# A one-layer hybrid recurrent decoder step on one core: x turned for the residual by VectorE, recurrent heads planned a unit sooner, a small product inside unit 1, one state load a slot later

## The chip, the cores and the metric

The kernel runs on one core of one Trainium2 chip. The metric is device time in microseconds for one execution. Three executions of the kernel before took 988.83, 991.7 and 995.17 us, median 991.7.

## What is computed

One step of a one-layer decoder trunk for a prompt of 512 tokens and a sample group of 8 sequences with 4 tokens each, so 544 token columns in all; the model width is 1024, everything is float32.

```python
def _layer(x, st, p):
    xn = rmsnorm(x, p['norm_mix_g'])
    proj = (xn @ p['w_in'] + p['b_in']).astype(f32)
    gq, gk, gv, gg, ga, mu, mi, mf, mo, rx, ry, gates = jnp.split(proj, ...)
    # GLA branch: lg = log_sigmoid(ga @ w_gla_a2 + b_gla_a2) / 16, chunked scan over q, k, v
    o_gla = head_rmsnorm(o, p['gla_norm_g'], 4) * jax.nn.silu(gg)
    # mLSTM branch: conv of mu, q/k/v, stabilised matrix memory C [v, k] for 4 heads
    o_m = head_rmsnorm(hm, p['mlstm_norm_g'], 4) * jax.nn.sigmoid(mo)
    # RG-LRU branch: conv of rx, r_g and i_g block-diagonal gates, linear recurrence
    hr, rh_new = rglru(xc, r_g, i_g, p['rglru_lambda'], rh)
    o_r = hr * jax.nn.gelu(ry)
    g3 = jax.nn.sigmoid(gates).reshape(B, L, 3, D_MODEL)
    mix = sum(g3[:, :, b] * (o_b @ wb_b) for b in range(3))
    x = x + mix @ p['w_out']
    xn2 = rmsnorm(x, p['norm_ffn_g'])
    uc, fconv_new = causal_dwconv(xn2 @ p['w_up'], fconv, ...)
    u_a, u_b = jnp.split(uc, 2, axis=-1)
    return x + (jax.nn.gelu(u_a) * u_b) @ p['w_down'], new_states
```

A final RMSNorm follows, and the new states of all branches are outputs too, for the prompt and for the 8 samples.

## The kernel before

Activations lie with features on the 128 partitions and the 544 tokens in the free dimension. The weights are worked off in **units**, numbered 0 to 120: a unit is one tile of 128 output features. Unit 0 holds the small projections, 1 to 8 q, k and v of GLA, 9 to 12 mu, 13 to 16 rx, 17 to 20 ry, 21 to 24 gg, 25 to 28 mo, 29 to 52 the three branches with their gates (24 units), 53 to 60 w_out (`U_OUT` is 53), then the feed-forward part (`U_UP`, `U_DOWN`).

A product is made of three float32r passes, high by high, low by high, high by low, over 8 tiles of 128 input features: 8 x 3 x 2 halves of 272 tokens = 48 matmuls. A unit of the branches has two products: the gate product (8 tiles, 48 matmuls) into PSUM pair 0, then the branch product (4 tiles, 24 matmuls) into pair 1.

For each unit u the work goes round five queues, each of which is strictly in its written order:
- **SP** loads the weights into one of two stage slots (`load`, L374) once GpSimd is through with unit u-2 (`free_stage`, semaphore `lo`).
- **ScalarE** casts them to the high part `whi` (`hi`, L1122; in loops L1131) once TensorE is through with unit u-2.
- **GpSimd** subtracts to the low part `wlo` (`lo`, L523), three instructions.
- **TensorE** makes the products (`gemm`, L602). Below unit 29 it waits for `evac` of unit u-2, that is, for ScalarE having emptied PSUM.
- **ScalarE** evacuates (`evac`, L1187 on). In the loop over u it does: wait for the product of u, `hi(u + 2)`, `evac(u)`, then the visits of u.

All else (recurrences, states, small products) is put between the units as **visits**: `plan(u, part, (what, k), ...)` says behind which unit (part 0) or between the two products of which unit (part 1) a step stands. Each engine has a function for each kind of step and calls it at that place of its own queue; steps of one unit come in the order in which they were planned. The steps that matter here:
- `a2`: TensorE's small product of `ga` with `wa2` (8 matmuls, L689), behind unit 1; ScalarE's `v_a2` takes its Abs twice (L1228), and then Abs, Exp and Ln of several rows.
- `rg` (TensorE L808 and ScalarE L1329 to L1338) and `rgd` (VectorE L1928 to L1946) for each recurrent head: TensorE makes two block-diagonal products, ScalarE Sigmoid twice, Tanh, Exp, Sqrt, VectorE the scan and the gated output `orh`, `orl`. ScalarE's step of head i waits for head i-1's gated output (`rg_o`); VectorE's raises `or`. Planned at units 24, 26, 28 and, between the products, 30.
- `gfin` (unit 24): VectorE makes the gated output of GLA, `ogh` and `ogl`, and raises `og` (L1904 to L1909); it waits for gg's last evacuation (unit 24). ScalarE stores the GLA states there.
- `rh` (unit 31, part 1): TensorE turns `rhn`, the new states of the recurrent branch, and waits for `or` of all four heads.
- `sH`, `sI` for h = 0 to 3: the sample step of mLSTM head h. `sH`: TensorE turns the state `ch_buf[h % 3]` in PSUM, ScalarE copies it to `cts` (L1418). `sI`: TensorE's products with `cts` (L911 to L915), VectorE's update, ScalarE's store of the new state. There are three buffers for four heads, so head 3's load waits for head 0's store (`ch_out`), in `sH(1)` on ScalarE.

The evacuation of unit 25, the first of mo, waits for `og`:

```python
i = u - U_MO
if i == 0:
    act.wait_ge(s("og"), 1)
    act.wait_ge(s("ss_new"), 2)
ins = func(split(mo[:, i, :]), src, ACT.Sigmoid, ...)   # L1219
```

TensorE begins unit 29 only after `evac` of all 29 units (`pe.wait_ge(s("evac"), U_GB)`).

Between units 53 and 54 TensorE turns x for the residual: x is loaded again in token order (`xp2`, `xs2`), 40 float32 turns go to PSUM pairs 2 and 3, and VectorE copies them to `xt` (L2126), one of eight tiles at a time. Behind the copies VectorE sets `up`, `fraw` and `ssa` to zero (L2127 to L2129). SP waits for `ssa`, loads the feed-forward convolution state into `fraw` (four loads, pieces of 128 bytes, L463), and goes on with the weights of unit 57. From unit 55 on TensorE waits for `x1`, VectorE's sum of `xt` and the product of two units before.

Of the kernel before, what the change touches and what calls it, by code (L numbers as in the profile page):

```python
# [13 lines left out]
P = 128  # L14
# [74 lines left out]
def layer(nc, io):  # L89
    ctx = ExitStack()  # L90
    with ctx:
# [72 lines left out]
        xs2 = at("xs2", [TS, D_MODEL], o)  # L164
# [10 lines left out]
        xp2 = at("xp2", [P, 4, D_MODEL], w0 + 8 * TB)  # L175
# [186 lines left out]
        def _(sp):  # L362
# [70 lines left out]

            for n in range(3):
# [5 lines left out]
                def pair_of_units(i):  # L440
                    for r in range(2):
                        slot = (u0 + r) % 2
                        free_stage(i * 2 + (u0 + r))
                        load(slot, one(gates, i * 2 + r), KT_IN)
                        sp.dma_start(stage[:, slot, KT_IN:KT_GB], one(outs, i * 2 + r)).then_inc(s(f"branch{slot}"), 16)

                done = 0
                if n == 2:
                    done = 2
                    for i in range(done):  # L450
                        pair_of_units(i)
# [134 lines left out]
        def _(pe):  # L586
# [507 lines left out]
        def _(act):  # L1094
# [1231 lines left out]
```

## Time and profile before

| What | Value |
|---|---|
| Median of three executions | 991.7 us (988.83 to 995.17) |
| Profiled execution | 993.07 us, span of its core 991.3 us |
| Mean granted TensorE clock | 0.991 |
| TensorE matmuls | 969.4 us busy, 98% |
| VectorE / ScalarE / GpSimd | 539.4 / 402.8 / 310.8 us busy |
| DMA | 89.62 MB, mean 90 GB/s |
| SP's queue, hardware_dynamic | 154341 packets, 79.16 MB |

TensorE is busy nearly all the time, so the numbers to look for are its few gaps, what released it behind each, and the clock that it was granted there. The other engines have slack on average, but they hold TensorE where one of them is late with the low part of the weights, with an evacuation or with a visit. In a timeline row the columns are the start in us from the span's start, the duration, engine and line, operation, output and inputs, the count of instructions merged into the row, and in brackets how long the engine was idle before it and what released it.

### The profile page before, as it was taken

How to read it: one execution, taken by the hardware profiler on the slowest of the kernel's cores; microseconds unless marked ns; L12 is line 12 of the kernel's file. 1: busy time of each engine (PE TensorE's matmuls, PEld its weight loads, DVE VectorE, ACT ScalarE, POOL GpSimd, SP SyncE). 2: the span in 40 equal slices, each digit the busy share in tenths (PEclk: the TensorE clock that was granted, in tenths of full speed). 3: DMA queues.
4: the chain of work that ended last, by engine and by line, in shares of the span. 5: the costliest groups of instructions: out<-in, count | busy, mean ns of one | idle time of the engine just before them, and what ended most of it. 6: DMA issues, size and time to landing. Idle time of an engine off the chain costs nothing.

```text
span 991.3 us, 19378 instructions
## 1 busy us (share of the span) xinstructions
PE 969.4 (98%) x7550; PEld 948.7 (96%) x7550; DVE 539.4 (54%) x906; ACT 402.8 (41%) x584; POOL 310.8 (31%) x301
## 2 busy tenths in 40 slices
PE   9999999999799999899999999999999999999997
PEld 8899999898799999899999999999999999999996
DVE  5586346677725357764225467776777777312122
ACT  5632433477525555123232344444444444222122
POOL 2653433245322234333543530010000000244440
PEclk9999999999999999999999999999999999999998
DMA  5235423244122223526224422333222223533222
GB/s 149 65 86 117 108 65 81 64 111 128 47 72 64 65 64 87 159 63 209 73 65 61 103 85 85 89 94 93 85 85 85 85 85 101 122 93 88 87 59 91
DMA packets 172018, 89.62 MB, mean 90 GB/s; under 512 B 13662, under 2 KB 169956, under 8 KB 171967
## 3 DMA queue, kind: packets, MB, share of 16 engines
q1 hardware_dynamic: 154341, 79.16, 29.0%
q10 hardware_dynamic: 17626, 9.74, 3.8%
q8 instruction: 37, 0.61, 0.2%
q14 instruction: 14, 0.11, 0.0%
HBM read 82.29 MB, written 6.32 MB: 89 GB/s over the span
## 4 chain that ended last, share of the span: by engine, by line
PE 44%; issue 35%; POOL 18%; ACT 1%; DMA 1%; POOLq 0%; DVE 0%; DVEq 0%
PE ps L602 42%; POOL wlo L523 18%; PE ps L1040 1%; PE ps L591 1%; DMA xtok<-x_prompt 1%; PE ps L661 0%; ACT junk L1144 0%; PE ps L627 0%; POOLq L557 0%; PE ps L620 0%; ACT xtok L1160 0%; PE ps L1031 0%; PE ps L1032 0%; ACT whi L1122 0%; POOL blkc L513 0%
## 5 line engine op out<-in xcount | busy, mean ns | idle before, releaser
L523 POOL TENSOR_TENSOR wlo<-stage,whi 128x384 fp32r<-128x384 f32 (+3 forms) x231 | 278.3, 1232 | 428.2 <-ACT whi L1122 332.7
L602 PE MATMUL ps<-xh,whi 128*128 128x272 f32 x1536 | 322.6, 291 | 4.0 <-POOL wlo L523 3.4
L602 PE MATMUL ps<-xh,wlo 128*128 128x272 f32 x1536 | 318.6, 289 | 0.0
L602 PE MATMUL ps<-xl,whi 128*128 128x272 f32 x1536 | 317.7, 288 | 0.0
L602 PEld LDWEIGHTS ps<-xh,whi 128*128 128x128 f32 x1536 | 242.8, 189 | 9.1 <-ACT qk L1201 2.5
L602 PEld LDWEIGHTS ps<-xl,whi 128*128 128x128 f32 x1536 | 242.0, 189 | 0.0
L602 PEld LDWEIGHTS ps<-xh,wlo 128*128 128x128 f32 x1536 | 240.5, 189 | 0.0
L1122 ACT ACTIVATE whi<-stage 128x1024 fp32r<-128x1024 f32 (+3 forms) x59 | 72.1, 1222 | 148.3 <-PE ps L602 131.2
L1131 ACT ACTIVATE whi<-stage 128x1024 fp32r<-128x1024 f32 (+1 forms) x54 | 59.9, 1109 | 147.3 <-PE ps L602 142.0
L575 POOL COPY up<-fst 128x16 f32 (+1 forms) x44 | 25.7, 586 | 227.9 <-DVE ca L2182 227.1
L2182 DVE SCALAR_TENSOR_TENSOR ca<-up,par,ca 128x560 f32<-128x560 f32 x88 | 70.3, 799 | 6.1 <-DVE ca L2182 3.2
L602 PE MATMUL ps<-hh,whi 128*128 128x272 f32 x330 | 69.0, 291 | 0.0
L602 PE MATMUL ps<-hl,whi 128*128 128x272 f32 x330 | 68.2, 287 | 0.0
L602 PE MATMUL ps<-hh,wlo 128*128 128x272 f32 x330 | 68.1, 288 | 0.0
L2172 DVE TENSOR_TENSOR wlo<-stage,whi 128x1024 fp32r<-128x1024 f32 (+1 forms) x44 | 54.7, 1243 | 10.0 <-ACT whi L1131 6.0
L2222 DVE TENSOR_TENSOR yb<-xt,ps 128x544 f32<-128x544 f32 x7 | 5.0, 721 | 87.3 <-PE ps L602 87.3
L602 PEld LDWEIGHTS ps<-hl,whi 128*128 128x128 f32 x330 | 52.1, 188 | 0.0
L602 PEld LDWEIGHTS ps<-hh,whi 128*128 128x128 f32 x330 | 51.5, 188 | 0.1
L602 PEld LDWEIGHTS ps<-hh,wlo 128*128 128x128 f32 x330 | 51.6, 188 | 0.0
L1464 ACT ACTIVATE sg<-ps,par 128x544 f32<-128x544 f32 x24 | 17.1, 714 | 80.3 <-PE ps L602 74.4
L2162 DVE TENSOR_TENSOR up<-ps,rstd 128x272 f32<-128x272 f32 x44 | 19.4, 442 | 53.0 <-PE ps L602 53.0
L2106 DVE TENSOR_TENSOR sg<-sg,ps 128x544 f32<-128x544 f32 x16 | 11.5, 719 | 59.1 <-PE ps L602 56.5
(440 smaller groups left out, 1350.7 us busy)
## 6 DMA issues: line engine op xcount, KB each, us to landing
stage<-w_in SPq DMA_DIRECT2D x52, 512.0 KB, 3.9
stage<-w_up SPq DMA_DIRECT2D x44, 512.0 KB, 3.7
stage<-w_down SPq DMA_DIRECT2D x16, 704.0 KB, 4.4
stage<-w_branch SPq DMA_DIRECT2D x24, 256.0 KB, 4.2
stage<-w_out SPq DMA_DIRECT2D x8, 512.0 KB, 3.5
ch<-state_mlstm_C ACTq DMA_DIRECT2D x4, 512.0 KB, 4.2
s_mlstm_C<-ch ACTq DMA_DIRECT2D x4, 512.0 KB, 4.2
xp<-x_prompt SPq DMA_DIRECT2D x1, 2048.0 KB, 9.8
```

What stands on the lines that cost most here:

```text
L523: ins = pool.tensor_tensor(wlo[:, slot, a:b, 0:n], stage[:, slot, a:b, 0:n], whi[:, slot, a:b, 0:n].bitcast(F32), ALU.subtract)
L575: pool.tensor_copy(fsam(row[:, FPW:PADF])[:, :, 0:FW - 1], fs).then_inc(s("pads"), 1)
L591: return nc.tensor.transpose(out, in_, ident[0:k, 0:k])
L602: ins = mm(dst[:, r, :], w[:, slot, k0 + k, :], x(k)[:, r * HT:(r + 1) * HT], start=first and k == 0 and q == 0, stop=last and k == n - 1 ...
L1040: ins = mm(halves(1)[:, r, :], w[:, slot, k, :], x[:, KT_DOWN + k, r * HT:(r + 1) * HT], start=False, stop=k == KT_DOWN - 1 and q == 2)
L1122: func(whi[:, slot, 0:kt, 0:n], stage[:, slot, 0:kt, 0:n], ACT.Copy).then_inc(s("hi"), 1)
L1131: func(whi[:, slot, 0:kt], stage[:, slot, 0:kt], ACT.Copy).then_inc(s("hi"), 1)
L1464: func(split(sg[:]), halves(0), ACT.Sigmoid, bias=col).then_inc(s("gate_ev"), 1)
L2106: v.tensor_tensor(split(sg[:]), split(sg[:]), halves(1), ALU.mult).then_inc(s("br_mul"), 1)
L2162: v.tensor_tensor(row[:, FW - 1:FW - 1 + HT], src[:, 0, :], rstd[:, 0:HT], ALU.mult)
L2172: v.tensor_tensor(wlo[:, slot, 0:kt], stage[:, slot, 0:kt], whi[:, slot, 0:kt].bitcast(F32), ALU.subtract)\
L2182: v.scalar_tensor_tensor(out=out, in0=row[:, t:t + CONVF], scalar=par[:, bass.ds(j + (P_FW + 2 * NF * t + NF * r), 1)], in1=out, op0=ALU.m ...
```

## The change

Four edits.

1. The small product `a2` is made by TensorE inside unit 1, behind its first four tiles, and ScalarE's two Abs of it stand in a function of their own that is called ahead of the wait for unit 1's product.
2. The four recurrent heads are planned at units 23, 25, 27 and 29, all in part 0. `gfin` stays at unit 24.
3. The load of head 3's mLSTM state, with its wait for head 0's store, moves from `sH(1)` to `sI(1)` on ScalarE.
4. x for the residual isn't turned by TensorE any more. SP loads it into `xq` in blocks of 32 by 32, with the feature blocks already on their partitions: 32 loads of 64 KB for the prompt and 4 of 32 KB for the samples, in pieces of 128 bytes, placed behind the weights of units 49 to 54. VectorE turns each of the eight tiles with its transpose of 32 x 32 blocks, from SBUF to `xt`. The wait for `om` stands ahead of unit 49's load, and the wait for all four `ch_out` there is gone.

```diff
-        plan(24, 0, ("gfin", 0))
-        for i in range(3):
-            plan(24 + 2 * i, 0, ("rg", i), ("rgd", i))
-        plan(30, 1, ("rg", 3))
-        plan(30, 0, ("rgd", 3))
+        for i in range(4):
+            plan(23 + 2 * i, 0, ("rg", i), ("rgd", i))
+        plan(24, 0, ("gfin", 0))
...
+            def tokens_in(k):
+                for a in range(4):
+                    part = io["x_prompt"][0].rearrange("(j t) (k a f) -> k a t j f", t=32, a=4, f=32)[k, a]
+                    dst = xq[32 * a:32 * a + 32, k, 0:SEQ].rearrange("p (j f) -> p j f", f=32)
+                    sp.dma_start(dst, part).then_inc(s("late_in"), 16)
+                if k < 4:
+                    part = io["x_sample"].rearrange("b t (k a f) -> a (b t) k f", a=4, f=32)[k]
+                    sp.dma_start(xq[32 * k:32 * k + 32, :, SEQ:T], part).then_inc(s("late_in"), 16)
...
-                    sp.wait_ge(s("om"), 1)
-                    sp.wait_ge(s("ch_out"), 64)
-                    sp.dma_start(xp2[:], io["x_prompt"][0].rearrange("(t p) d -> p t d", p=P)).then_inc(s("late_in"), 16)
-                    sp.dma_start(xs2[:], io["x_sample"].rearrange("b t d -> (b t) d")).then_inc(s("late_in"), 16)
...
+            sp.wait_ge(s("om"), 1)
+            for q in range(4):
+                unit_in(2 + q // 2, q % 2)
+                tokens_in(q)
+            for q in range(2):
+                free_stage(U_OUT + q)
+                load((U_OUT + q) % 2, one(tiles(w_out, 0, KD), q), KT_IN)
+                tokens_in(4 + 2 * q)
+                tokens_in(5 + 2 * q)
+            load_all(U_OUT + 2, tiles(w_out, 2 * P, KD - 2), 2, KT_IN)
...
-                if u >= 2:
-                    pe.wait_ge(s("evac"), u - 1)
+                if u == 1:
+                    pe.wait_ge(s("lo"), 2)
+                    gemm(halves(1), 1, 0, 4, x_of(xh), x_of(xl), last=False)
+                    v_a2(0)
+                    gemm(halves(1), 1, 4, 4, x_of(xh, 4), x_of(xl, 4), first=False).then_inc(s("gemm"), 1)
+                    continue
+                pe.wait_ge(s("evac"), u - 1)
...
-            pe.wait_ge(s("late_in"), 32)
             pe.wait_ge(s("state_rows"), 5)
             pe.wait_ge(s("m3_copied"), NMC + 1)
-            for j in range(KD):
-                if j >= 2:
-                    pe.wait_ge(s("xt"), j - 1)
-                for t in range(4):
-                    tr(pair(2 + j % 2)[:, t * P:(t + 1) * P], xp2[:, t, j * P:(j + 1) * P], P)
-                tr(pair(2 + j % 2)[:, SEQ:T], xs2[:, j * P:(j + 1) * P], TS).then_inc(s("xt_tr"), 1)
...
-                if h == 1:
-
-                    act.wait_ge(s("ch_out"), 16)
-                    act.dma_start(ch_buf[0][:], io["state_mlstm_C"][0].rearrange("b h v k -> h v b k")[3])\
-                       .then_inc(s("ch_in3"), 16)
                 act.wait_ge(s("ch_tr"), h + 1)
...
             def v_sI(h):
                 if h == H - 1:
                     rms_of(NMC, TS)
+                if h == 1:
+                    act.wait_ge(s("ch_out"), 16)
+                    act.dma_start(ch_buf[0][:], io["state_mlstm_C"][0].rearrange("b h v k -> h v b k")[3])\
+                       .then_inc(s("ch_in3"), 16)
                 act.wait_ge(s("ch_new"), h + 1)
...
             for u in range(U_GB):
+                if u == 1:
+                    a2_abs()
                 act.wait_ge(s("gemm"), u + 1)
...
             dve.wait_ge(s("stored"), 4)
+            dve.wait_ge(s("late_in"), 576)
             for j in range(KD):
-                dve.wait_ge(s("xt_tr"), j + 1)
-                v.tensor_copy(xt[:, j, :], pair(2 + j % 2)[:, 0:T]).then_inc(s("xt"), 1)
+                v.transpose(xt[:, j, :], xq[:, j, :]).then_inc(s("xt"), 1)
+            dve.wait_ge(s("xt"), KD)
```

## Rows read from the trace of the kernel before

**Rows 1.** The page, busy us of each engine, share of the span, instructions.

```profile
PE 969.4 (98%) x7550; PEld 948.7 (96%) x7550; DVE 539.4 (54%) x906; ACT 402.8 (41%) x584; POOL 310.8 (31%) x301
```

**Rows 2.** Timelines of TensorE and ScalarE behind unit 1 and ahead of unit 4.

```profile
33.26 2.10 PE L689 MATMUL ps<-ga,wa 16*128 16x272 f32 x8
35.39 1.32 ACT L1228 ACTIVATE g<-ps,par 128x544 f32<-128x544 f32 x2 [0.15 <-PE ps L689]
49.54 0.49 PE L602 MATMUL ps<-xh,whi 128*128 128x272 f32 x2 [1.96 <-POOL wlo L523]
```

**Rows 3.** Windows: stretch, us, busy PE, PEld, DVE, ACT, POOL, clock, DMA, GB/s.

```profile
51.50:53.50 2.00, 2.00 (x11) 2.00 (x11) 1.83 (x7) 0.96 (x2) 0.72 (x1) 0.50 0.58 169
224.00:225.10 1.10, 0.00 (x1) 0.03 (x1) 1.07 (x4) 0.30 (x1) 1.10 (x2) 1.00 0.00 0
```

**Rows 4.** Timeline of TensorE in unit 31: the turn of rhn and what follows.

```profile
271.90 1.02 PE L591 MATMUL ps<-ident,rhn 128*9 128x128 f32 x4 [5.53 <-DVE orl L1946]
277.36 2.00 PE L829 MATMUL ps<-mcv,wq 128*128 128x272 f32 x8
```

**Rows 5.** Timelines of ScalarE and TensorE in the sample step of head 1.

```profile
408.92 1.02 ACT L1418 ACTIVATE cts<-ps 128x1024 f32<-128x1024 f32 x1 [4.48 <-DMA s_mlstm_C<-ch]
409.99 3.33 PE L911 MATMUL ps<-cts,qbm 128*32 128x129 f32 x16 [2.53 <-ACT cts L1418]
```

**Rows 6.** Timelines of four engines around units 53 to 57, and VectorE's transpose.

```profile
502.57 26.35 SPq L374 DMA_DIRECT2D stage<-w_out  x4
526.17 1.32 DVE L2120 TENSOR_TENSOR ml<-mix,mh  x1 [0.83 <-ACT mh L1491]
535.33 1.49 DVE L2126 COPY xt<-ps 128x544 f32<-128x544 f32 x2 [0.16 <-PE ps L591]
549.91 1.06 ACT L1131 ACTIVATE whi<-stage 128x1024 fp32r<-128x1024 f32 x1 [5.34 <-DMA stage<-w_out]
554.75 0.52 PE L602 MATMUL ps<-mh,whi 128*128 128x272 f32 x2 [0.41 <-POOL wlo L523]
583.02 1.63 DVE L2153 STREAM_TRANSPOSE fst<-fraw 128x1408 f32<-128x1408 f32 x1
```

**Rows 7.** Timeline of ScalarE: cast of unit 26, head 0's gates, unit 25's evacuation.

```profile
208.64 1.04 ACT L1122 ACTIVATE whi<-stage 128x1024 fp32r<-128x1024 f32 x1
212.24 1.28 ACT L1329 ACT_TABLE_LOAD   x1 [1.95 <-issue]
222.04 0.71 ACT L1219 ACTIVATE mo<-ps,par 128x544 f32<-128x544 f32 x1
```

**Rows 8.** Timeline of VectorE: gfin, then heads 0, 1 and 3.

```profile
210.32 4.39 DVE L1904 SCALAR_TENSOR_TENSOR gv<-gv,par,gg 128x544 f32<-128x544 f32 x4 [4.97 <-ACT gg L1213]
...
216.07 2.43 DVE L1909 TENSOR_TENSOR ogl<-gv,ogh 128x2176 fp32r<-128x2176 f32 x1
...
219.89 0.75 DVE L1931 SCALAR_TENSOR_TENSOR rt<-rt,rt 128x568 f32<-128x568 f32 x1 [0.73 <-ACT rt L1338]
...
227.48 1.41 DVE L1946 TENSOR_TENSOR orl<-rt,orh 128x544 fp32r<-128x544 f32 x1
...
232.66 0.75 DVE L1931 SCALAR_TENSOR_TENSOR rt<-rt,rt 128x568 f32<-128x568 f32 x1 [3.10 <-ACT rt L1338]
...
239.41 1.27 DVE L1942 TENSOR_TENSOR rt<-rt,ry 128x32 f32<-128x32 f32 x1
...
242.21 1.70 DVE L1946 TENSOR_TENSOR orl<-rt,orh 128x544 fp32r<-128x544 f32 x1
...
263.74 0.75 DVE L1931 SCALAR_TENSOR_TENSOR rt<-rt,rt 128x568 f32<-128x568 f32 x1 [1.94 <-ACT rt L1338]
...
271.13 0.72 DVE L1946 TENSOR_TENSOR orl<-rt,orh 128x544 fp32r<-128x544 f32 x1
```

**Rows 9.** Windows of the fraw loads, then of one unit's weights.

```profile
542.00:546.00 4.00, 4.00 (x34) 4.00 (x33) 2.69 (x3) 2.25 (x3) 2.54 (x3) 1.00 1.52 71
549.00:550.00 1.00, 1.00 (x10) 1.00 (x9) 0.18 (x1) 0.09 (x1) 0.00 (x0) 1.00 1.12 336
```

More of the change, by code:

```diff
@@ L163, in layer @@
         pm = at("pm", [P, 4, PADM], o)
-        xs2 = at("xs2", [TS, D_MODEL], o)
         o += RXB
@@ L174, in layer @@
         dt_ = at("dt", [P, 5, P], w0 + 20480)
-        xp2 = at("xp2", [P, 4, D_MODEL], w0 + 8 * TB)
+        xq = at("xq", [P, KD, T], w0 + 8 * TB)
         rows = [at(f"row{i}", [4, 553], w0 + i * RB) for i in range(9)]
@@ L438, in _, with unit_in @@
                 u0 = U_GB + KD * n
-                def pair_of_units(i):
-                    for r in range(2):
[L442 to L451, printed above, removed]
-                    sp.wait_ge(s("om"), 1)
-                    sp.wait_ge(s("ch_out"), 64)
-                    sp.dma_start(xp2[:], io["x_prompt"][0].rearrange("(t p) d -> p t d", p=P)).then_inc(s("late_in"), 16)
-                    sp.dma_start(xs2[:], io["x_sample"].rearrange("b t d -> (b t) d")).then_inc(s("late_in"), 16)
-                with sp.Fori(done, KD // 2) as i:
-                    pair_of_units(i)
-            load_all(U_OUT, tiles(w_out, 0, KD), 4, KT_IN)
+                def unit_in(i, r):
+                    slot = (u0 + r) % 2
+                    free_stage(i * 2 + (u0 + r))
+                    load(slot, one(gates, i * 2 + r), KT_IN)
+                    sp.dma_start(stage[:, slot, KT_IN:KT_GB], one(outs, i * 2 + r)).then_inc(s(f"branch{slot}"), 16)
+                with sp.Fori(0, KD // 2 if n < 2 else 2) as i:
+                    for r in range(2):
+                        unit_in(i, r)
+            sp.wait_ge(s("om"), 1)
[8 more added lines that the diff above has]
+            load_all(U_OUT + 2, tiles(w_out, 2 * P, KD - 2), 2, KT_IN)
             sp.wait_ge(s("ssa"), 1)
@@ L1222, in _, with a2_abs @@
             a2v = ps[:, 2048:4096].rearrange("p (j a b) -> p j a b", j=2, a=2)[:, :, :, 0:HT]
-            def v_a2(_):
+            def a2_abs():
                 act.wait_ge(s("a2"), 1)
@@ L1228, in v_a2 @@
                     func(split(g1[:, j, :]), a2v[:, j], ACT.Abs, bias=par[:, P_A2 + j:P_A2 + j + 1]).then_inc(s("a2_act"), 1)
+            def v_a2(_):
                 act.wait_ge(s("a2_act"), 2)
@@ L2151, in _ @@
                     residual(i, r)
-            dve.wait_ge(s("late_in"), 96)
+            dve.wait_ge(s("late_in"), 640)
             v.transpose(fst[:].rearrange("p f c -> p (f c)"), fraw[:].rearrange("p f c -> p (f c)")).then_inc(s("fst"), 1)
@@ L2248, in _ @@
             output(1, 1, U_DOWN + 3)
-            dve.wait_ge(s("late_in"), 112)
+            dve.wait_ge(s("late_in"), 656)
             gained(0, 0, 0)
```

## The prediction, made before the changed kernel ran

> **What bounds the kernel now.** I read the page's engine shares first: TensorE is busy 969.4 of 991.3 us with 7550 matmuls [rows 1], 0.128 us each, so a unit of 48 full matmuls is 6.1 us and one of 72 is 9.2 us. All other engines have slack on average, so time can come only from matmuls removed, from gaps in TensorE's row, or from its clock. Then I read TensorE's timeline for gaps. Those that this change touches are 1.96 us ahead of unit 4 [rows 2], 1.1 us ahead of unit 27 [rows 3], 5.53 us inside unit 31, where the states of the recurrent branch are turned [rows 4], 2.53 us in the sample step of head 1 [rows 5] and 0.41 us ahead of unit 57 [rows 6]. Last I read windows: two microseconds after the 1.96 us gap TensorE runs at a granted clock of 0.50, that is 1.2 instead of 2.4 GHz; the 1.1 us gap before 225.1 is passed at 1.00 [rows 3]. The clock has a price in rows: behind the 5.53 us gap four turns and 24 matmuls take 271.90 to 277.36, 5.5 us, where 28 at 0.128 and the turns' start make about 3.7: 1.8 us. Behind the 2.53 us gap sixteen matmuls take 3.33 us instead of 2.0: 1.3 us [rows 4, 5]. The question is whether each edit leaves TensorE free, or makes a longer wait elsewhere.
>
> **1. Small product inside unit 1.** The product (8 matmuls, 2.10 us) ran behind unit 1; now it splits the unit. TensorE does the same work. ScalarE's two Abs (1.32 us, and a wait of 0.15 ahead of them) come off the stretch between unit 1's end and ScalarE's cast for unit 4, but unit 1 ends 2.0 us later, and all of that stretch starts there. The cast moves 2.0 - 1.5 = 0.5 us later, and so does unit 4, which waits for the low part behind it [rows 2]. The wait is not removed: **+0.5 us** (0 to +1).
>
> **2. Recurrent heads a unit sooner.** The aim is plain: the last head ends sooner, so the 5.53 us gap goes. But each queue is in order, and head 0 now stands ahead of two things that it used to follow: the ScalarE work of unit 24 and VectorE's end of the gated branch (gfin). Step by step:
> - ScalarE is through with unit 23's SiLUs at 208.6; there it cast the weights of unit 26. Head 0's gates took 212.24 to 219.8 (VectorE's next step was released by their last) = 7.5 us, three table loads in them [rows 7, 8]. Now they come first: 208.7 to 216.2, and only then unit 26's cast and unit 24's evacuation.
> - VectorE did gfin 210.32 to 218.50 (8.2 us), while ScalarE made the gates, and then head 0 from 219.89 to 228.89 (9.0 us) [rows 8]. Now it waits for the gates until 216.2, does head 0 until 225.3, and gfin until 233.5.
> - gfin raises "og". ScalarE's evacuation of unit 25 waits for og (line 1217), as its output lies over buffers of the gated branch. Before, og stood at 218.5 and the evacuation ran at 222.04 [rows 7, 8]. Now: 233.5 + a table load 1.3 + 0.7 = 235.7. TensorE's unit 27 needs it and starts at 235.9 instead of 225.1. Behind the same wait stand head 1's gates and the cast for unit 28.
> - Head 1's gates, 7.5 less one table load = 6.2 us, now run 235.7 to 241.9. The cast (1.0) and unit 26's evacuation (2.0 with its table) follow; with its low part unit 28 starts near 246.8. VectorE's head 1 reached its gated output 8.0 us after its gates (232.66 to 240.68) [rows 8]: now 250.0. Head 2's gates wait for that: 250.2 to 256.4. They now stand ahead of unit 30's cast (1.5 for half as many columns again) and of unit 28's evacuation (2.0): 259.9. Unit 29 waits for that: 260.1.
> - Unit 28 ended near 252.9, so that is a gap of 7 us, and the clock falls, as behind the 5.53 us gap [rows 4]: +1.8. From 260.1: gate product 6.1 + 1.8, branch product 3.1, head 3's product 2.0, unit 30 9.2, gate product of unit 31 6.1 = 288.4. Head 3 runs under it: gates 273 to 279.2, VectorE 9.0 more. So the turn starts at 288.4, with no wait or almost none, instead of at 271.90 [rows 4]: +16.5. The half clock behind it is gone: -1.8. Sum **+14.7 us**.
>
> Bounds: a head on VectorE took from 8.1 us (263.74 to 271.85) to 11.3 us (232.66 to 243.91) [rows 8]. With short ones (0.9 less for head 0, some 2 less on head 1's way to its output) and no fall of the clock part 2 is +10; with a long head 0 it is +17.
>
> **3. Load of the fourth head's state a slot later.** ScalarE stood 4.48 us for the store of head 0's state to land before it copied cts; TensorE's 2.53 us gap is that [rows 5]. With the wait moved behind the copy, cts is written right after the turn, ahead of TensorE's need at 407.5. The load is then issued about when the store lands (408.4, as before), and its buffer is needed two heads later. Gap and half clock go: **-3.8 us** (-2.5 to -4).
>
> **4. x turned by VectorE.** 40 turns leave TensorE; paced by VectorE's eight copies of 0.75 us, they held it a little over 6 us. The last copy of xt ended at 536.82. Now VectorE can start after its last ml (527.49). A transpose of 1408 columns took 1.63 us, so one of 544 takes 0.63, eight 5.1: done at 532.6, 4.2 us sooner. Behind it hang the memsets, ssa, SP's loads of fraw and, in the same queue, the weights of unit 57, for which ScalarE waited 5.34 us until 549.9 [rows 6]. TensorE arrives over 6 us sooner, that load only 4.2. Unit 57 starts at 550.6 instead of 554.75, behind a gap of some 2.5 us. Gaps of 1.96, 2.53 and 5.53 us cost clock, 1.1 did not; I take the fall: -4.2 + 1.8 = **-2.4 us** (-4.2 without it; -1 if GpSimd's work slows the transposes by half).
> SP now issues 36 loads in place of 2. x comes in pieces of 128 bytes, 2.2 MB in all, four to eight loads behind each unit's weights from unit 49 on. The nearest row is fraw's, also of 128 bytes: 71 GB/s, against 336 in a stretch of weights [rows 9]. Unit 53's weights went out at 502.57 [rows 6], unit 54's 9 us later. Behind each come 0.52 MB of x, 7.4 us, and 1.6 for the weights: the last lands near 523.5, against 527.5 when VectorE asks. Hidden by 4 us; the weights between them are asked for no sooner. I take nothing.
> The Trainium skill ("DMA: Bandwidth & Descriptors", Specifications) gives 512 B as the least transfer that reaches line rate and says that smaller ones are read, changed and written back. The trace agrees with 71 GB/s in fraw's stretch. It speaks against this edit, as the second rival does.
>
> **Sum.** 0.5 + 14.7 - 3.8 - 2.4 = +9.0 us on the span of 991.3. The profiled execution took 993.07, 1.4 over the median of 991.7; the difference is put on the median: **1000.7 us**, 0.9% slower.
>
> **Rivals.**
> - *It does what it is for (faster).* Place: og against unit 27. If VectorE is through gfin by the time TensorE ends unit 26 (about 225), nothing in part 2 waits, and 5.53 + 1.8 + 1.1 go: the sum is 0.5 - 8.4 - 3.8 - 2.4 = -14.1: 977.6 us. Against it: head 0 stands before gfin in VectorE's queue, and the two took 17.2 us, from gates that can't be ready before 216 [rows 7, 8]. For it: only that I read the order wrongly. 0.13.
> - *Loads of 128 bytes are late.* If they run under 56 GB/s (1.05 MB in the 21.9 us from 503.6 to 525.5, less 3.2 for weights), the transposes, x1 and unit 55 wait. At 40 GB/s that is 7.5 us: 1008.2. For it: consecutive pieces of x lie 128 KB apart in memory, fraw's 512 bytes. Against: 4 us of slack at fraw's rate [rows 9]. 0.13.
> - *The chain of part 2 is right but short* (+10, clock keeps up): 0.5 + 10 - 3.8 - 4.2 = +2.5: 994.2. 0.12.
> - The forecast, with its own range 996 to 1006: 0.62.
>
> By the Trainium skill ("TensorE: Matmul & The Clock Gate", Part 1) the full clock is something that activity releases and idleness takes back, so each gap is paid twice; the trace agrees behind the gaps of 1.96, 2.53 and 5.53 us.
>
> **From cases to numbers.** A measurement of this kernel can tell about 1% (9.9 us) from no change. Of the forecast's 0.62 some 0.25 lies over 1001.6; with most of the late loads (0.12) slower gets 0.37. Faster is the first rival: 0.13. Within 1%: 0.50. The range 992 to 1010 holds the forecast, the short chain and half of the late loads; it leaves out 977 and the far end of the loads.
>
> **What would show it.** Right: VectorE's gv (gfin) starts after orl of head 0; og near 233; the first mo at 235 behind a long wait on VectorE; gaps of 9 us ahead of unit 27 and 7 us ahead of unit 29, with a clock near 0.50 behind them; no wait at the turn of rhn; no wait of L911 on cts; unit 4 still waits; a gap of 2 to 3 us ahead of unit 57, released by GpSimd behind a load of w_out. Wrong: gfin done before 225; a wait of VectorE's transposes for x; an unbroken row of TensorE from 200 to 290.

## The result, and the profile after

The changed kernel takes 994.3 us (median of 20 executions, 992.4 to 995.5) against 990.6 us for the kernel before (20 executions, 988.7 to 995.2). The ratio is 1.0035, with a 95% interval of 1.0026 to 1.0044: some 3.5 us slower. The forecast was 9.0 us slower. The sign was right and the time lies in the range, but the size was 2.5 times too large. The experiments show that two terms of the sum were mis-sized: part 2 cost 11.1 us inside the change and not 14.7, and part 4 gave 4.8 and not 2.4.

The page of the changed kernel (engine shares: busy us, share of the span, matmuls):

```profile
PE 965.9 (97%) x7510; PEld 947.6 (95%) x7510; DVE 536.1 (54%) x906; ACT 404.0 (41%) x585; POOL 311.4 (31%) x301
```

and the view of TensorE's waits (waiting line, releaser: us in all, times, longest):

```profile
PE ps L611 <- POOL wlo L532: 9.1, 5, 3.7
PE ps L611 <- ACT mo L1227: 8.7, 2, 5.2
```

The 40 turns of x are gone from TensorE (7510 matmuls against 7550 in [rows 1]), yet it waits 17.8 us in its two largest groups. Most of that is new and lies between units 25 and 29. (Lines behind the change are shifted: L602 of before is L611, L1219 is L1227.)

**Part 2 in the trace after.** Timeline, first TensorE, then ScalarE and VectorE (start, us, engine, line, in brackets the idle time ahead and its releaser):

```profile
222.08 0.79 PE L611 MATMUL ps<-xh,whi 128*128 128x272 f32 x2 [3.73 <-POOL wlo L532]
234.56 0.52 PE L611 MATMUL ps<-xh,whi 128*128 128x272 f32 x2 [3.50 <-ACT mo L1227]
245.94 0.49 PE L611 MATMUL ps<-xh,whi 128*128 128x272 f32 x2 [1.65 <-POOL wlo L532]
257.40 0.82 PE L611 MATMUL ps<-xh,whi 128*128 128x272 f32 x2 [5.20 <-ACT mo L1227]
285.66 0.60 PE L600 MATMUL ps<-ident,rhn 128*9 128x128 f32 x4
289.12 2.00 PE L838 MATMUL ps<-mcv,wq 128*128 128x272 f32 x8
...
209.25 1.28 ACT L1339 ACT_TABLE_LOAD   x1
216.68 1.04 ACT L1130 ACTIVATE whi<-stage 128x1024 fp32r<-128x1024 f32 x1
232.50 1.28 ACT L1227 ACT_TABLE_LOAD   x1 [11.45 <-DVE ogl L1920]
...
225.78 2.86 DVE L1915 SCALAR_TENSOR_TENSOR gv<-gv,par,gg 128x544 f32<-128x544 f32 x4
230.00 2.42 DVE L1920 TENSOR_TENSOR ogl<-gv,ogh 128x2176 fp32r<-128x2176 f32 x1
```

This is the chain that was forecast. Head 0's gates start at 209.25 and the cast for unit 26 stands behind them, at 216.68 instead of 208.64. VectorE comes to gfin at 225.78, og is there at 232.4, and ScalarE stands 11.45 us for it. TensorE starts unit 27 at 234.56 and unit 29 at 257.40. The turn of rhn has no wait any more, but it starts at 285.66 instead of 271.90, and the product behind it at 289.12 instead of 277.36 [rows 4]: 11.8 us later, 0.3 of which came from part 1.

Windows of the same trace (stretch, its length, busy PE, PEld, DVE, ACT, POOL, granted clock, DMA share, GB/s), with two of part 1 and one behind the gap ahead of unit 57:

```profile
35.00:37.00 2.00, 2.00 (x11) 2.00 (x10) 0.46 (x1) 0.00 (x0) 0.00 (x0) 0.50 0.66 199
51.70:53.70 2.00, 1.99 (x16) 2.00 (x17) 1.97 (x3) 0.65 (x1) 2.00 (x3) 1.00 0.37 86
222.00:226.00 4.00, 3.92 (x17) 3.95 (x18) 3.93 (x5) 0.00 (x0) 3.27 (x3) 0.50 0.57 148
257.40:259.40 2.00, 2.00 (x9) 2.00 (x10) 1.97 (x3) 0.00 (x0) 2.00 (x2) 0.50 0.00 0
556.50:558.50 2.00, 1.99 (x15) 1.99 (x16) 1.39 (x2) 1.15 (x2) 1.97 (x2) 1.00 0.31 93
```

Behind the gaps ahead of units 26 and 29 TensorE runs at 1.2 GHz, and so it does from 235.0 to 238.4, behind the gap ahead of unit 27.

**Parts 1, 3 and 4 in the trace after.** The same timelines:

```profile
30.46 2.07 PE L698 MATMUL ps<-ga,wa 16*128 16x272 f32 x8 [0.16 <-DVE kes L1694]
45.80 1.04 ACT L1130 ACTIVATE whi<-stage 128x1024 fp32r<-128x1024 f32 x1
51.71 0.49 PE L611 MATMUL ps<-xh,whi 128*128 128x272 f32 x2 [2.43 <-POOL wlo L532]
...
405.86 1.96 PE L920 MATMUL ps<-cts,qbm 128*32 128x129 f32 x16
...
535.03 5.12 DVE L2137 STREAM_TRANSPOSE xt<-xq 128x544 f32<-128x544 f32 x8
541.81 0.51 DVE L2141 MEMSET ssa<- 128x544 f32 x1
542.35 2.88 SPq L472 DMA_DIRECT2D fraw<-state_ffn_conv  x4
545.59 11.41 SPq L372 DMA_DIRECT2D stage<-w_out  x3
551.68 1.06 ACT L1139 ACTIVATE whi<-stage 128x1024 fp32r<-128x1024 f32 x1 [4.41 <-DMA stage<-w_out]
556.51 0.52 PE L611 MATMUL ps<-mh,whi 128*128 128x272 f32 x2 [1.15 <-POOL wlo L532]
```

Unit 4 still waits, 2.43 us instead of 1.96. This time the clock stays at 1.00 behind it; it fell earlier, inside unit 1 (35 to 37), behind the small product. The products on cts run without a wait, 1.96 us instead of 3.33. The eight transposes take 5.12 us as estimated and start at once, with no wait for x: its last load had landed at 526.60, 8.4 us before. Unit 57 waits 1.15 us. Counted by TensorE's row in the two traces, the start of unit 57 is 1.8 us later than before, where the shift was 7.6 us ahead of it.

### The profile page after: what moved, and what is told of

Its sections match the earlier page's. It is cut to its first block, busy times and chain, and to the rows that moved or that the text cites. A ratio compares the mean times of both kernels' runs of the same rounds, so it can differ in the third digit from the quotient of the medians.

```text
span 993.0 us, 19319 instructions
## 1 busy us (share of the span) xinstructions
PE 965.9 (97%) x7510; PEld 947.6 (95%) x7510; DVE 536.1 (54%) x906; ACT 404.0 (41%) x585; POOL 311.4 (31%) x301
## 4 chain that ended last, share of the span: by engine, by line
PE 44%; issue 35%; POOL 18%; ACT 1%; DMA 1%; POOLq 0%; DVE 0%; DVEq 0%
PE ps L611 42%; POOL wlo L532 18%; PE ps L1048 1%; PE ps L600 1%; DMA xtok<-x_prompt 1%; PE ps L670 0%; ACT junk L1152 0%; PE ps L636 0%; POOLq L566 0%; PE ps L629 0%; ACT xtok L1168 0%; PE ps L1039 0%; PE ps L1040 0%; ACT whi L1130 0%; POOL blkc L522 0%
## 5 line engine op out<-in xcount | busy, mean ns | idle before, releaser
L611 PE MATMUL ps<-xh,whi 128*128 128x272 f32 x1536 | 325.3, 293 | 16.7 <-ACT mo L1227 8.7
L611 PE MATMUL ps<-xh,wlo 128*128 128x272 f32 x1536 | 320.6, 290 | 0.0
L611 PE MATMUL ps<-xl,whi 128*128 128x272 f32 x1536 | 320.1, 290 | 0.0
L611 PEld LDWEIGHTS ps<-xh,whi 128*128 128x128 f32 x1536 | 245.2, 191 | 22.0 <-ACT mo L1227 11.2
L611 PEld LDWEIGHTS ps<-xl,whi 128*128 128x128 f32 x1536 | 244.5, 191 | 0.0
L611 PEld LDWEIGHTS ps<-xh,wlo 128*128 128x128 f32 x1536 | 243.2, 191 | 0.0
L611 PE MATMUL ps<-hh,whi 128*128 128x272 f32 x330 | 69.0, 291 | 0.0
L611 PE MATMUL ps<-hl,whi 128*128 128x272 f32 x330 | 68.1, 287 | 0.0
L611 PE MATMUL ps<-hh,wlo 128*128 128x272 f32 x330 | 68.0, 287 | 0.0
L611 PEld LDWEIGHTS ps<-hl,whi 128*128 128x128 f32 x330 | 52.0, 188 | 0.0
L611 PEld LDWEIGHTS ps<-hh,wlo 128*128 128x128 f32 x330 | 51.5, 188 | 0.0
L611 PEld LDWEIGHTS ps<-hh,whi 128*128 128x128 f32 x330 | 51.5, 188 | 0.1
L2117 DVE TENSOR_TENSOR sg<-sg,ps 128x544 f32<-128x544 f32 x16 | 11.5, 719 | 56.6 <-PE ps L611 54.0
```

Source lines behind the costliest of these rows:

```text
L611: ins = mm(dst[:, r, :], w[:, slot, k0 + k, :], x(k)[:, r * HT:(r + 1) * HT], start=first and k == 0 and q == 0, stop=last and k == n - 1 ...
L2117: v.tensor_tensor(split(sg[:]), split(sg[:]), halves(1), ALU.mult).then_inc(s("br_mul"), 1)
```

## Experiments

Each run has the kernel before on the same chip. For one quantity I use all executions of a kernel: its span, and the loss to the clock, which is one minus the mean granted clock, times the span. "At full clock" is the span less that loss. The clock is given to 0.001, so one value is good to half a microsecond. The measure counts a stretch at half clock whether TensorE works in it or not, so it overstates what the clock cost. In every trace the clock is at 0.50 in the last 3.7 to 6.6 us of the span, when TensorE has no work left; these 1.9 to 3.3 us of loss cost nothing and differ from one execution to the next. The end of the first trace of before, in the columns of the windows above:

```profile
986.40:991.30 4.90, 0.00 (x0) 0.00 (x0) 0.22 (x1) 0.00 (x0) 0.00 (x0) 0.50 0.67 241
```

**Each part alone, or taken back.** Part 2 taken back (the other three stay):

```diff
-        for i in range(4):
-            plan(23 + 2 * i, 0, ("rg", i), ("rgd", i))
         plan(24, 0, ("gfin", 0))
+        for i in range(3):
+            plan(24 + 2 * i, 0, ("rg", i), ("rgd", i))
+        plan(30, 1, ("rg", 3))
+        plan(30, 0, ("rgd", 3))
```

> The changed kernel with the recurrent heads back in their old units (parts 1, 3 and 4 remain). Theory A (the ledger of the two traces: part 1 +0.3, part 2 +11.5, part 3 -4.1, part 4 -5.9 us, and the parts add up): 991 - 9.7 = about 981 us, ratio 0.990. Theory B (as the record before the run had it: parts 3 and 4 give only 6.2 together with part 1 costing 0.5, and what the trace shows as more is one execution's luck): 991 - 5.7 = 985.5, ratio 0.994.

Measured: 983.2 us, ratio 0.992 (0.990 to 0.995). The interval holds both theories. By the ratios part 2 cost 11 us of the changed kernel (1.0035 - 0.9923) and the others gave 7.6. The traces gave 9.7 for them; the difference is that the first trace of before lies 2.5 us over its median of 990.6, and the trace of the changed kernel 0.5 over its own (below).

Part 2 alone, the same lines of the plan the other way round in the kernel before:

> The kernel before with part 2 alone (heads a unit sooner). Theory A: +11.5 us, ratio 1.0116: og near 232, gaps ahead of units 26, 27 and 29 with a clock near 0.5 behind them, no wait at the turn of rhn. The prediction on record had +14.7, ratio 1.0148.

Measured: 1004.4 us, ratio 1.014 (1.011 to 1.017), which holds both. The trace has gaps of 3.73, 3.72 and 5.20 us ahead of units 26, 27 and 29 and none at the turn. By the ratio part 2 costs 14.2 us alone, near the forecast, and 11 inside the change. Trace against trace it is the same both times: 11.1 us of span alone (1002.4 against 991.3), 11.2 inside (993.0 against 981.8).

Part 4 alone (the loads of xq, VectorE's transposes, no turns on TensorE):

> The kernel before with part 4 alone (x for the residual turned by VectorE). Theory A (ledger of the traces): -5.9 us, ratio 0.994, with a gap of 1 to 1.5 us ahead of unit 57 and no fall of the clock behind it. Theory B (as predicted: gap 2.5 us and half clock): -2.4 us, ratio 0.9975. If loads of 128 bytes held something up: 1.000 or more.

Measured: 985.7 us, ratio 0.994 (0.992 to 0.997), with 0.65 us ahead of unit 57 and a clock of 1.00 behind it. The interval holds 5.9 and just leaves out 2.4.

Parts 3 and 1 alone:

> The kernel before with part 3 alone (state load of the fourth head behind the copy). Theory A: the gap of 2.5 to 2.8 us goes in every execution, and 1.7 us of clock in those in which it fell there: -2.5 to -4.2, ratio 0.996 to 0.9975. As predicted: -3.8. Rival (the load, issued later, is late for head 3): a new wait there and ratio 1.000.

> The kernel before with part 1 alone (small product inside unit 1). As predicted: unit 4 starts 0.5 us later, ratio 1.0005. Theory A: the gap ahead of unit 4 is 2.4 instead of 2.0 us, and the clock falls once in this stretch, inside unit 1 or behind unit 4: +0.5 to +2.2 us by how often the kernel before is spared the fall, ratio 1.000 to 1.002.

Measured: 988.2 us, 0.9966 (0.9948 to 0.9983) for the load, as forecast; 991.9 us, 1.0026 (1.0002 to 1.0049) for the product; that interval holds both of its theories. Its ten executions span 988.4 to 995.8 us at clocks of 0.996 to 0.986.

**The kernel before, traced again.** No edit.

> The kernel before, once more, for a second trace. The first trace loses 1.7 us of clock behind unit 4's gap, 3.4 behind the gap at the turn of rhn and 1.7 behind the gap in head 1's sample step. Theory A (whether the clock falls behind a gap of 2 to 2.5 us differs from one execution to the next): one or two of the three are missing here, and the span is shorter by 1.7 us for each, 987 to 990. Theory B (the falls belong to the kernel): the same three, span 991.

Timeline of TensorE at two gaps, and windows behind three, of this second execution:

```profile
49.44 0.49 PE L602 MATMUL ps<-xh,whi 128*128 128x272 f32 x2 [1.96 <-POOL wlo L523]
407.71 1.96 PE L911 MATMUL ps<-cts,qbm 128*32 128x129 f32 x16 [2.71 <-ACT cts L1418]
```

```profile
51.40:53.40 2.00, 2.00 (x19) 2.00 (x18) 1.83 (x7) 0.96 (x2) 0.72 (x1) 1.00 0.66 194
269.80:271.80 2.00, 2.00 (x10) 1.78 (x11) 0.00 (x0) 0.59 (x1) 0.00 (x0) 0.50 1.12 330
407.70:409.70 2.00, 1.99 (x17) 1.77 (x18) 0.97 (x2) 1.33 (x1) 0.59 (x1) 1.00 0.83 229
```

The first trace has, in the stretch behind its gap of 2.53 us:

```profile
410.00:412.00 2.00, 2.00 (x10) 1.65 (x11) 1.14 (x2) 1.31 (x1) 0.61 (x1) 0.50 0.81 235
```

The same program, the same gaps, 1.96 us both times and 2.71 against 2.53. The first execution fell to 0.50 behind both [rows 3], the second behind neither; behind the gap of 5.53 us both fell. Spans: 991.3 and 987.1. By the measure above a fall counts 1.7 us, or 3.4 where the clock came back later, but part of that can be idle time. At the turn of rhn in the first trace the clock is at 0.50 from 269.5 on, and TensorE waits until 271.90:

```profile
269.50:271.90 2.40, 0.00 (x0) 0.00 (x0) 2.28 (x5) 0.00 (x0) 0.39 (x1) 0.50 0.27 55
271.90:276.30 4.40, 4.39 (x20) 4.18 (x21) 0.00 (x0) 0.59 (x1) 0.00 (x0) 0.50 0.56 158
```

So this fall counts 3.4 us and cost 2.2, half of the 4.4 us in which TensorE worked; the forecast's 1.8 was near. Theory A holds: of the losses that the forecast priced, the two smaller ones are a matter of the single execution.

Over the executions listed with their clock, with the parts alone and taken back (us, means):

| kernel | executions | span | loss to the clock | at full clock |
|---|---|---|---|---|
| before | 54 | 989.3 | 7.0 | 982.3 |
| changed | 20 | 992.4 | 11.7 | 980.7 |
| part 1 alone | 10 | 991.3 | 8.4 | 982.8 |
| part 2 alone | 4 | 1003.0 | 13.8 | 989.2 |
| part 3 alone | 10 | 986.3 | 6.7 | 979.6 |
| part 4 alone | 5 | 983.2 | 7.1 | 976.1 |
| changed without part 1 | 12 | 991.6 | 11.7 | 979.9 |
| changed without part 2 | 4 | 981.5 | 7.6 | 973.9 |
| changed without part 3 | 6 | 997.7 | 14.8 | 982.9 |
| changed without part 4 | 6 | 998.0 | 12.6 | 985.3 |

At full clock the parts alone give +0.5, +6.9, -2.7 and -6.2, together -1.5, and the whole change gives -1.6. The losses don't add: +1.4, +6.8, -0.3 and +0.1 make 8.0, and the whole change lost 4.7 more. The changed kernel is faster than before at full clock and slower by the clock. The traces say the same when only the time is counted in which TensorE worked at half clock: it cost 8.9 us in the changed kernel and 5.4 and 1.8 in the two traces of before, which leaves 984.2 against 986.0 and 985.3. The rows without parts 1, 3 and 4 come from three runs that take back one part each:

> The changed kernel without part 4 (x turned by TensorE again). Over their executions the runs so far split into span at full clock and loss to the clock (one minus the mean granted clock, times the span). Before 982.2 + 6.9; changed 980.7 + 11.7; part 1 alone +0.7 and +1.5; part 2 alone +7.0 and +6.9; part 3 alone -2.6 and -0.2; part 4 alone -6.1 and +0.2. Theory A (waits add up, losses to the clock don't): full-clock span +6.1 over the changed kernel, loss about the same 11.7: ratio to the kernel before 1.0095. As predicted on record (part 4 is worth 2.4): ratio 1.006.

> The changed kernel without part 3 (the state load of the fourth head ahead of the copy again). Theory A: full-clock span +2.6; the clock falls behind the gap of 2.8 us in nearly every execution, as in the trace with part 2 alone, where before it did so in some: +1.7, ratio 1.008. Theory B (losses to the clock are each kernel's chance and independent of the stage ahead): +2.6 and +0.5, ratio 1.0065.

> The changed kernel without part 1 (small product behind unit 1 again). Theory A: full-clock span -0.7, and the clock is lost in this stretch no oftener than in the kernel before: -1.0: ratio 1.002. As predicted on record: -0.5, ratio 1.003.

Measured: 999.8 us, 1.0083 (1.0057 to 1.0108); 998.8 us, 1.0079 (1.0050 to 1.0107); 993.1 us, 1.0021 (1.0005 to 1.0038). Inside the change part 4 gave 4.8 us, part 3 gave 4.4 and part 1 cost 1.4. With the 11.1 of part 2 that is +3.3, against 3.5 measured. So close a match is luck: by the mean spans of the table the four are -5.6, -5.4, +0.7 and +10.9, together +0.6 against 3.1. The last two ratios are theory A's and the first lies between theory A (1.0095) and the forecast (1.006), but each interval holds the other reading too. Where part 3 got more than alone can be seen in the kernel without it (timeline and window of TensorE in head 1's sample step):

```profile
422.11 2.86 PE L920 MATMUL ps<-cts,qbm 128*32 128x129 f32 x16 [2.83 <-ACT cts L1428]
```

```profile
423.00:425.00 2.00, 2.00 (x11) 1.36 (x10) 0.00 (x0) 0.43 (x1) 1.50 (x2) 0.50 0.46 137
```

The clock fell here, and in the trace of part 2 alone too. In the four traces that have this gap and the heads in their old units (two of the kernel before, part 1 alone, part 4 alone) it fell in one. Why it should fall oftener with the heads sooner, 150 us earlier, is not shown.

**Is it gfin?** The changed kernel with gfin planned ahead of head 0:

```diff
+        plan(23, 0, ("gfin", 0))
         for i in range(4):
             plan(23 + 2 * i, 0, ("rg", i), ("rgd", i))
-        plan(24, 0, ("gfin", 0))
```

> The changed kernel, but VectorE's end of the gated branch (gfin) planned ahead of head 0 in unit 23. Theory A (part 2 costs 11.5 us mainly because head 0 stands before gfin and og comes at 232 instead of 218): gfin runs under head 0's gates, og near 217, the wait of ScalarE's mo on og goes. Left are the gap of 3.7 us and the half clock at unit 26 (ScalarE casts its weights behind the gates), and some 2 us ahead of unit 29, whose start waits for the evacuation behind head 2's gates; the turn of rhn is free. Part 2 then costs about +1 (0 to +3): 993 - 10 = about 983, ratio 0.991. Rival (the loss is the order on ScalarE, gates ahead of the casts, and og only shares it): no change against the changed kernel, ratio 1.003.

Measured: 995.0 us, ratio 1.004 (1.001 to 1.006): nothing gained, as the rival said. Timelines of VectorE, ScalarE and TensorE:

```profile
218.41 5.30 DVE L1915 SCALAR_TENSOR_TENSOR gv<-gv,par,gg 128x544 f32<-128x544 f32 x4 [14.43 <-ACT gg L1221]
...
217.66 0.71 ACT L1221 ACTIVATE gg<-ps,par 128x544 f32<-128x544 f32 x1
...
219.20 0.79 PE L611 MATMUL ps<-xh,whi 128*128 128x272 f32 x2 [2.53 <-POOL wlo L532]
229.63 0.82 PE L611 MATMUL ps<-xh,whi 128*128 128x272 f32 x2 [2.72 <-ACT mo L1227]
243.78 0.79 PE L611 MATMUL ps<-xh,whi 128*128 128x272 f32 x2 [4.60 <-POOL wlo L532]
256.38 0.68 PE L611 MATMUL ps<-xh,whi 128*128 128x272 f32 x2 [3.68 <-ACT mo L1227]
```

gfin can't run under the gates: it needs the last gg, which ScalarE evacuates at 217.66, behind head 0's gates. og came 4.9 us sooner than in the changed kernel's trace, and so did unit 27; unit 28 came only 2.2 and unit 29 only 1.0 us sooner, since each then waited for a cast or an evacuation behind the next head's gates. This trace was 1.6 us ahead already at unit 23, as no clock had fallen in it by then; less that, unit 27 came 3.3 and unit 28 0.5 us sooner, and unit 29 0.6 later. Part 2's cost is that ScalarE's gates stand ahead of work that TensorE needs; og is the first of several such waits, not the cause.

**Can the 5.5 us gap go without moving heads?** With parts 1, 3 and 4, the turn of rhn moved down:

```diff
-        plan(31, 1, ("rh", 0))
-        plan(31, 0, ("mprep", 0), ("mqk", 0))
-        plan(32, 1, ("mqk", 1), ("mqk", 2))
-        plan(32, 0, ("mqk", 3))
+        plan(32, 1, ("rh", 0), ("mprep", 0), ("mqk", 0), ("mqk", 1))
+        plan(32, 0, ("mqk", 2), ("mqk", 3))
```

> Parts 1, 3 and 4, heads in their old units, and in addition the turn of rhn with the first q and k products moved from unit 31 to behind the gate product of unit 32 (9 us later in TensorE's row). Theory A (what part 2 was after can be had without moving a head, since nobody needs the turned states soon): the gap of 5.5 us and the half clock behind it go, 1.7 to 3.4 us: 983.2 - 7 to 9 = 974 to 976 us, ratio 0.985. Rival (the q and k products are needed at the chunk steps, and the wait only moves there): 981 to 983, ratio 0.992.

Measured: 979.6 us, ratio 0.989 (0.985 to 0.993), halfway. The timeline of TensorE shows new waits, 3.5 us with one of 0.42 not shown:

```profile
270.02 0.52 PE L611 MATMUL ps<-xh,whi 128*128 128x272 f32 x2 [0.58 <-POOL wlo L532]
277.62 2.07 PE L838 MATMUL ps<-mcv,wq 128*128 128x272 f32 x8 [0.88 <-issue]
281.28 2.07 PE L838 MATMUL ps<-mcv,wq 128*128 128x272 f32 x8 [1.60 <-ACT mq L1375]
```

By the measure of the table all of the gain is clock (4.6 us lost against 7.6, and 973.6 against 973.9 at full clock), but that measure counts the half clock inside the old gap as well. By the two traces TensorE waits 2.0 us less here (3.5 against 5.5) and loses 2.0 us less of its work to half clock; of the 4.0 us, 3.2 are left in its row behind this stretch; where the rest goes is not shown. The clock had fallen in the one gap of 5.5 us; behind the four small ones it did not.

Or only the last head sooner, with the turn in its old place:

```diff
-        plan(30, 1, ("rg", 3))
-        plan(30, 0, ("rgd", 3))
+        plan(29, 0, ("rg", 3), ("rgd", 3))
```

> Parts 1, 3 and 4, and of part 2 only the last head a unit sooner: heads 0 to 2 in their old units, head 3 behind unit 29 instead of inside unit 30. Theory A (gates cost where a cast or an evacuation that TensorE needs stands behind them; behind head 3's gates stands only the sigmoid of unit 30): gates of head 3 as soon as head 2's output is there (near 252.5), VectorE through near 266; TensorE waits 1 to 2 us for the sigmoid ahead of unit 31 and no longer at the turn of rhn: 983.2 - 5.5 + 1.5 - (1.7 to 3.4 of clock) = 976 to 977.5 us, ratio 0.986. Rival (any head sooner takes ScalarE from what TensorE needs, as in part 2): 983 or more, ratio 0.993.

Measured: 977.2 us, ratio 0.9875 (0.9855 to 0.9894), as theory A had it. Timelines of ScalarE and TensorE:

```profile
252.96 0.73 ACT L1340 ACTIVATE rt<-ps,par 128x568 f32<-128x568 f32 x1 [1.85 <-DVE rt L1954]
260.51 0.71 ACT L1476 ACTIVATE sg<-ps,par 128x544 f32<-128x544 f32 x1
...
261.37 0.48 PE L612 MATMUL ps<-xh,whi 128*128 128x272 f32 x2 [0.91 <-ACT sg L1476]
267.76 0.61 PE L601 MATMUL ps<-ident,rhn 128*9 128x128 f32 x4 [0.15 <-DVE orl L1958]
```

Behind these gates stands only one sigmoid, and TensorE waits 0.91 us for it instead of 5.53 at the turn. What part 2 was after is to be had from one head of the four.

**The two gaps that parts 1 and 4 left.** Weights of unit 57 asked for ahead of fraw (on the kernel without part 2, then on the one with the last head sooner), and ScalarE's logarithms moved behind the cast for unit 4:

```diff
+            free_stage(U_OUT + 4)
+            load(U_OUT % 2, one(tiles(w_out, 0, KD), 4), KT_IN)
             sp.wait_ge(s("ssa"), 1)
...
-            load_all(U_OUT + 4, tiles(w_out, 4 * P, KD - 4), KD - 4, KT_IN)
+            load_all(U_OUT + 5, tiles(w_out, 5 * P, KD - 5), KD - 5, KT_IN)
```

```diff
+            def a2_ln():
+                act.wait_ge(s("a2_act"), 3)
                 func(g1[:], g1[:], ACT.Ln, bias=one).then_inc(s("a2_act"), 1)
...
                 hi(u + 2)
                 evac(u)
+                if u == 2:
+                    a2_ln()
```

> Parts 1, 3 and 4 (heads in their old units), and the weights of unit 57 asked for ahead of the loads of fraw, without waiting for VectorE's memsets. Theory A (the 1.05 us gap ahead of unit 57 is what is left of part 4's gain, since these weights queue behind fraw's loads of 128 bytes): the gap goes, 983.2 - 1 = 982.2 us, ratio 0.9915; a difference that the traces show better than the times. Rival (the weights then delay fraw and something that needs it): 983 or more.

> The two preceding edits together: last head a unit sooner, weights of unit 57 ahead of fraw. If they add up: 1 us under the run with the last head alone, 975 to 976.5 us, ratio 0.985.

> The preceding kernel, and in addition ScalarE's logarithms of the decays (a table load and two operations, 3.2 us) moved behind the cast of unit 4's weights. Theory A (part 1 left the gap ahead of unit 4 standing because that cast waits for the logarithms): the cast runs near 42.8 instead of 45.8, the gap of 2.4 us goes, and the clock then falls at most once before unit 10: 2 to 4 us under the preceding kernel, 972 to 974 us, ratio 0.982. Rival (VectorE's scan, 2 us later, is late for the first chunk): the gain comes back as a wait before unit 12.

Measured: 980.0 us, 0.991 (0.9895 to 0.993), which the time can't tell from the 0.992 without this edit, but the trace has no gap left at unit 57; 975.7 us, 0.986 (0.984 to 0.988), 1.5 us under the last head alone; 973.0 us, 0.983 (0.982 to 0.985), which beats both kernels. Timeline of ScalarE in the last one, and its largest group of TensorE's waits:

```profile
42.24 1.06 ACT L1133 ACTIVATE whi<-stage 128x1024 fp32r<-128x1024 f32 x1 [0.65 <-PE ps L614]
45.22 1.21 ACT L1251 ACTIVATE g<-g,cst 128x1088 f32<-128x1088 f32 x1
```

```profile
PE ps L614 <- POOL wlo L535: 1.8, 4, 1.2
```

The cast runs at 42.24 (45.80 in the changed kernel, 46.18 in the preceding one), and unit 4 no longer waits: it starts 4.1 us sooner than in the preceding kernel's trace. Of these, 1.7 us come back by unit 10, with waits of 0.25 and 0.21 us for GpSimd's low parts and 0.60 us for VectorE's rows, so the rival had a small part of the truth. The mean span is 2.5 us under that of the preceding kernel, and 2.0 of it is loss to the clock (1.9 against 3.9), of which 0.7 lies, in the two traces, in the idle end of the span. No fall is left in this stretch. The one inside unit 1 came ahead of the gap, so that the gap is gone does not explain why it is absent. Its four executions lie within 0.8 us of each other, all at 0.998.

## Why the forecast was right or wrong

**Part 1 (forecast +0.5; measured +1.4 inside the change, +2.6 alone, interval 0.2 to 4.9).** The mechanism was right: unit 1 ends later, the cast too, and unit 4's wait stays; neither measurement excludes 0.5. Unit 4's start moved by 2.17 us, 1.7 of which is half clock inside unit 1, where the clock fell although TensorE had waited only 0.16 us. I had taken the loss to the clock behind unit 4 as part of the kernel on both sides. In the changed kernel's trace the fall inside unit 1 came in its place; by the end of unit 8 the shift was 0.2. This is chance to a large part: of the eleven traces with part 1 the clock fell inside unit 1 in four, behind unit 4 in three and at neither place in four, and never at both; of the six without it, it fell behind unit 4 in five.

**Part 2 (forecast +14.7; measured +14.2 alone, +11.1 inside the change).** This is the first mis-sized term. The order of events came as written: head 0 ahead of gfin, og at 232.4 (forecast 233.5), unit 27 at 234.56 (235.9), unit 28 at 245.94 (246.8), unit 29 at 257.40 (260.1), from there to the turn 28.3 us (28.3), the turn free. The step that failed is VectorE's durations, which make the 2.7 us at unit 29: gfin took 6.6 us and not 8.2, and head 1 reached its output in 6.9 us and not 8.0. Both were carried over from stretches of before in which GpSimd worked. Beside gfin it was idle now. Beside head 1 it worked both times, on pieces of 512 columns before and of 256 and 384 now, and the scan took 2.38 and 2.09 us; that the pieces are the cause is not shown. I had also put one wait of 9 us ahead of unit 27, where my own times (about 225 to 235.9) make 10.9. It came as 3.73 us ahead of unit 26 (the late cast, whose time I had worked out but not carried to TensorE) and 3.50 ahead of unit 27, and in between unit 26 took 2.9 us longer at half clock, 10.1 in all. So that fall only shortened the wait behind it. That og is what costs was too narrow a reading: in the run with gfin first og came at 227.5 instead of 232.4, and nothing was gained. The first rival's condition, gfin done before 225, was reached in no run with head 0 sooner; that it would not have been enough, with the gates still ahead of the casts, is likely by this run and not shown.

In the two traces part 2 is worth 11.5 us. That the run alone gave 14.2, near the forecast, is no hit for it. Its trace too lies only 11.1 us over that of before; the rest is that the kernel before is often spared falls of the clock (a mean loss of 7.0 us, against 8.9 in its first trace), and this one is not (13.8 on the mean, 14.0 in its trace).

**Part 3 (forecast -3.8; measured -3.4 alone, -4.4 inside).** Right. With part 2 present the clock fell at this gap in both traces, without it in one of four.

**Part 4 (forecast -2.4; measured -5.7 alone, -4.8 inside, -5.9 in the traces).** This is the other mis-sized term, and it has two halves, the gap ahead of unit 57 and the clock behind it. VectorE's side was right: ssa came 4.2 us sooner, counted against the shift. But the weights of unit 57 landed 9.3 us behind the end of ssa (551.68 - 542.32) and not 11.0 as before (549.91 - 538.87), which I had carried over. The six traces of kernels without part 4 have 10.1 to 11.1 there and the eight with it, and with these weights behind fraw, 8.9 to 9.7, so it goes with the edit; why is open. So the gap was 1.15 us, not 2.5. And I had added 1.8 us for a fall of the clock behind it. It fell in none of the traces with this part, at gaps of 0.65 to 1.42 us. The forecast took as certain a fall behind each gap of two microseconds or more, and put its own gap of 2.5 us among them.

**The sum.** 0.5 + 14.7 - 3.8 - 2.4 = 9.0 was forecast; inside the change it is 1.4 + 11.1 - 4.4 - 4.8 = 3.3 (each from two ratios with intervals of 0.1 to 0.3%). Of the miss of 5.7, part 2 is 3.6, part 4 2.4 and part 3 0.6; part 1 took 0.9 back. The two steps that failed are thus VectorE's durations in part 2's chain, and in part 4 the time from ssa to the weights of unit 57 with a fall of the clock that did not come. The falls did not cancel either, as the sum of part 2 had them (+1.8 and -1.8): by the table part 2 added 4.1 us of loss to the clock inside the change and 6.8 alone, beside 6.8 and 6.9 at full clock.

**The rivals.** The loads of 128 bytes were not late: VectorE's transposes followed ml at once, with 8.4 us of slack where the forecast had 4. The Trainium skill ("DMA: Bandwidth & Descriptors", Specifications) gives 512 B as the least transfer that reaches line rate. Fraw's stretch agrees, with 71 GB/s [rows 9], but these loads were under cover, as the forecast took them. "The chain right but short" at 994.2 is what came nearest: part 2 near +11, and no fall of the clock behind unit 57's gap, though it did fall behind unit 29's. That its time is within 0.1 us of the measured 994.3 is partly luck, since it was reckoned from a median of 991.7 and the kernel before came at 990.6. I gave it 0.12 because I took for exact the durations that came from busy stretches, and for certain the falls.

## What to carry to other kernels

Before moving a step up in an in-order queue, list what then stands behind it and when each other engine needs that: moving the one head behind which nothing urgent stood gained 4.8 us by the ratios, and moving all four cost 11. Price a wait at its length, and the clock behind it as a chance and not a sum; trace the kernel before twice, since a mean clock that differs between executions says that the first trace is one draw. Durations that go into a chain should come from a stretch where the neighbouring engines do what they will do there.

## What the runs showed of the hardware that was not expected

- The clock does not fall behind every gap of 2 us. Behind 1.96 and 2.5 to 2.7 us it fell in one execution of the kernel before and not in another; behind 2.43 us in the changed kernel it did not, in the same kernel without part 3 it did. In the changed kernel it fell inside unit 1, in an unbroken row of matmuls, 1.1 us behind eight small products on 16 rows that had followed a wait of 0.16 us. At the gap of 5.5 us ahead of the turn of rhn it fell in all seven traces that have this gap. The kernel before spans 986.9 to 994.6 us at mean clocks of 0.996 to 0.987, and the best kernel, which has hardly a gap, 971.0 to 971.8 at 0.998.
- VectorE's four operations of gfin, each with two inputs in SBUF, took 2.86 us in all where GpSimd was idle, 4.39 [rows 8] and 5.30 where it made low parts of weights. Windows of these stretches, first of the changed kernel, then of the one with gfin first (the busy time just ahead of the clock is GpSimd's):

```profile
225.80:228.60 2.80, 2.80 (x16) 2.80 (x15) 2.80 (x5) 0.00 (x0) 0.00 (x0) 0.58 0.76 195
```

```profile
218.50:223.70 5.20, 4.50 (x24) 4.53 (x25) 5.20 (x4) 0.82 (x1) 4.28 (x4) 0.67 0.41 104
```

The Trainium skill ("SBUF — State Buffer", Who interferes with whom) has a VectorE instruction with two SBUF inputs contend with a GpSimd instruction that reads SBUF. The traces agree: 0.7 us for one such operation alone, 1.3 beside GpSimd's subtraction.
